# Expert layers: 16-bit one-hots laid out for adjacent pairs, and no tile of zeros

## The reference, cut to what matters

```python
def peer_ffn(x, w_q, sub_keys, exp_u, exp_v):
    q = (x @ w_q).reshape(B, T, PEER_HEADS, 2, PEER_DKEY // 2)
    s = jnp.einsum('bthcd,hcnd->bthcn', q, sub_keys)       # 8 heads, 2 sides, 128 keys
    top_s, top_i = lax.top_k(s, PEER_TOPK)                 # 16 of each side
    cand_s = top_s[..., 0, :, None] + top_s[..., 1, None, :]
    best_s, pos = lax.top_k(cand_s.reshape(..., 256), PEER_TOPK)
    idx = row * 128 + column                               # of the expert picked
    gate = jax.nn.softmax(best_s, axis=-1)
    h = jax.nn.gelu(jnp.einsum('md,mkd->mk', xb, exp_u[ib]))
    return jnp.einsum('mk,mkd->md', gb * h, exp_v[ib])     # 128 picks per token
```

## Time and profile before

| what | value |
|---|---|
| median of 3 runs | 3005.61 us |
| the runs | 3006.25, 2999.36, 3005.61 us |
| the profiled execution's own time | 2999.36 us |
| its span in the profile | 2997.6 us |
| PE busy, matmuls | 2594.2 us (87%) |
| PE busy, weight loads | 2419.3 us (81%) |
| DVE busy | 1988.2 us (66%) |
| ACT busy | 1347.4 us (45%) |
| POOL busy | 643.0 us (21%) |

### The profile page before, as it was taken

One profiled execution on the slowest core, in us unless ns is written; L12 is line 12 of the kernel. 1 busy time (PEld: TensorE's weight loads), 2 busy tenths in 40 slices (PEclk: granted clock), 3 DMA queues, 4 the chain that ended last, 5 costly groups with the idle time before them and its releaser, 6 DMA issues. The chain is left out here.

```text
span 2997.6 us, 61808 instructions
## 1 busy us (share of the span) xinstructions
PE 2594.2 (87%) x22240; PEld 2419.3 (81%) x22240; DVE 1988.2 (66%) x4119; ACT 1347.4 (45%) x2439; POOL 643.0 (21%) x506
## 2 busy tenths in 40 slices
PE   5798677798399589999999999866899999999998
PEld 2598556468397588999988899865899999988997
DVE  5501632341652469599999966546596899999765
ACT  5632334234320265655544455523555555444554
POOL 0144124227200379100000000162593000000000
PEclk9899779799696799999999999987999999999999
DMA  9522012115100234544434355421344544443452
GB/s 302 179 91 79 1 39 75 59 57 156 42 1 1 72 132 163 180 157 155 161 141 146 140 180 184 136 89 36 128 168 168 169 154 154 145 148 141 171 193 98
DMA packets 153851, 374.20 MB, mean 125 GB/s; under 512 B 8656, under 2 KB 102880, under 8 KB 137088
## 3 DMA queue, kind: packets, MB, share of 16 engines
q1 hardware_dynamic: 150784, 367.59, 36.1%
q10 hardware_dynamic: 2944, 4.98, 0.5%
HBM read 371.49 MB, written 1.05 MB: 124 GB/s over the span
## 5 line engine op out<-in xcount | busy, mean ns | idle before, releaser
L2413 ACT ACTIVATE w_hi<-ring 128x512 fp32r<-128x512 f32 x1024 | 643.6, 631 | 779.7 <-PE bank L2468 417.4
L2419 DVE TENSOR_TENSOR w_lo<-ring,w_hi 128x512 fp32r<-128x512 f32 x864 | 572.2, 690 | 207.7 <-ACT w_hi L2413 194.7
L360 POOL TENSOR_TENSOR w_lo<-ring,w_hi 128x512 fp32r<-128x512 f32 (+2 forms) x264 | 328.5, 1258 | 1340.4 <-ACT w_hi L351 1328.8
L2450 PE MATMUL bank<-x_hi,w_hi 128*128 128x256 f32 x2048 | 591.8, 289 | 20.4 <-POOL w_lo L2419 19.7
L2468 PE MATMUL bank<-hidden_hi,w_hi 128*128 128x256 f32 x2048 | 579.4, 283 | 34.3 <-issue 21.4
L2450 PE MATMUL bank<-x_lo,w_hi 128*128 128x256 f32 x2048 | 579.2, 283 | 0.0
L2450 PE MATMUL bank<-x_hi,w_lo 128*128 128x256 f32 x2048 | 578.9, 283 | 0.0
L2468 PE MATMUL bank<-hidden_hi,w_lo 128*128 128x256 f32 x2048 | 569.7, 278 | 0.0
L2468 PE MATMUL bank<-hidden_lo,w_hi 128*128 128x256 f32 x2048 | 569.2, 278 | 0.0
L2468 PEld LDWEIGHTS bank<-hidden_hi,w_hi 128*128 128x128 f32 x2048 | 383.8, 187 | 45.9 <-issue 29.9
L2450 PEld LDWEIGHTS bank<-x_hi,w_hi 128*128 128x128 f32 x2048 | 392.8, 192 | 24.2 <-ACT w_hi L2413 18.0
(11 more groups left out here) (519 smaller groups left out, 4460.8 us busy)
## 6 DMA issues: line engine op xcount, KB each, us to landing
ring<-in_peer_uT SPq DMA_DIRECT2D x128, 1024.0 KB, 4.9
ring<-in_peer_v SPq DMA_DIRECT2D x128, 1024.0 KB, 4.8
ring<-in_even_w_in SPq DMA_DIRECT2D x26, 1024.0 KB, 5.2
ring<-in_ada_w SPq DMA_DIRECT2D x24, 1024.0 KB, 8.8
ring<-in_odd_w_in SPq DMA_DIRECT2D x12, 1024.0 KB, 5.3
ring<-in_even_w_out SPq DMA_DIRECT2D x8, 1024.0 KB, 5.1
ring<-in_odd_w_out SPq DMA_DIRECT2D x8, 1024.0 KB, 5.1
ring<-in_peer_w_q SPq DMA_DIRECT2D x8, 1024.0 KB, 5.4
```

Source lines behind the costliest of these rows:

```text
L360: eng.tensor_tensor(k.lo[g % PARTS][:, 0:n], src, k.hi[g % PARTS][:, 0:n].bitcast(F32), ALU.subtract).then_inc(k.lo_ready, 1)
L2413: act.activation(k.hi[q][:, :], k.ring[slot][:, q * PART:q * PART + PART], ACT.Copy).then_inc(k.hi_ready, 1)
L2419: eng.tensor_tensor(k.lo[q][:, :], k.ring[slot][:, q * PART:q * PART + PART], k.hi[q][:, :].bitcast(F32), ALU.subtract).then_inc(k.lo_read ...
L2450: mm = pe.matmul(k.bank[s][:, j * T:j * T + T], a[q][:, w], b[:, cc, :], start=(cc == 0 and n == 0), stop=(cc == KC - 1 and n == 2))
```

## The change

It does six things.

1. `iota` moves from a tile of its own to the last 128 numbers of `hidden`. It is copied by DVE, once for each layer, to two bf16 tiles: `iota1` (0, 1, 2, ...) and `iota2` (0, 0, 1, 1, 2, 2, ...).
2. `rowT` holds each row index twice side by side. The one-hot of the row keeps its layout (token, row), and compares bf16 with bf16, with adjacent pairs innermost.
3. `hot` and `right` are laid out with the token innermost: (column, token) and (part, column, token). The one-hot of the column compares `iota2` with `colT`, pairs of tokens innermost.
4. `gateT` is laid out (part, token) and not (token, part).
5. PE's gate matmul takes as moving data `right[:, g, part, :, t]`: 64 columns, four elements (8 bytes) apart. Before they were adjacent.
6. The tile of zeros, its memset and the 16 matmuls of each layer are gone. The first matmul of each bank in column 0 of G2 starts the sum, the last of D ends it. For this the first round of G2 and the last of D are written out in place of a pass of the loop. DVE's last additions wait for `consumed`, the count of the parts that PE has used.

```diff
-        self.right = fold(small(2, GROUP, 3, HALF_J), "g t q j", g=2, t=GROUP, q=3)
-        self.hot = fold(small(GROUP, HALF_J), "t j", t=GROUP)
-        self.rowT, self.colT = small(T), small(T)
-        self.gateT = fold(small(T, 3), "t q", q=3)
-        self.zero = small(T)
+        self.right = fold(small(2, 3, HALF_J, GROUP), "g q j t", g=2, t=GROUP, q=3)
+        self.hot = fold(small(HALF_J, GROUP), "j t", t=GROUP)
+        self.rowT = fold(small(T, 2), "t c", c=2)
+        self.colT = small(T)
+        self.gateT = fold(small(3, T), "q t", q=3)
...
-                for a, b in ((k.hi, self.hh), (k.hi, self.hl), (k.lo, self.hh)):
-                    mm = pe.matmul(out, a[q][:, w], b[:, j, :], start=False, stop=False, skip_group_check=True)
+                for n, (a, b) in enumerate(((k.hi, self.hh), (k.hi, self.hl), (k.lo, self.hh))):
+                    mm = pe.matmul(out, a[q][:, w], b[:, j, :], start=first and cc % 2 == 0 and n == 0,
+                                   stop=last and cc % 2 == 1 and n == 2, skip_group_check=True)
...
-                mm = pe.matmul(k.bank[4 + g][:, t * HALF_J:(t + 1) * HALF_J], self.left[:, g, t, :], self.right[:, g, t, part, :],
+                mm = pe.matmul(k.bank[4 + g][:, t * HALF_J:(t + 1) * HALF_J], self.left[:, g, t, :], self.right[:, g, part, :, t],
...
-        self.zeros(pe, True)
-        with pe.Fori(0, ROUNDS) as r:
+        for n in range(STEPS):
+            self.dense_gates(pe, 2 * ROUNDS, n)
+            self.down_column(pe, 2 * ROUNDS, n // PAIR, n % PAIR, first=n == 0)
+        with pe.Fori(1, ROUNDS) as r:
...
-        with pe.Fori(0, ROUNDS) as r:
+        with pe.Fori(0, ROUNDS - 1) as r:
...
-        self.zeros(pe, False).then_inc(self.summed, 1)
+        for n in range(STEPS):
+            self.down_column(pe, 4 * ROUNDS - 1, n // PAIR, n % PAIR, last=n == STEPS - 1)
...
-        S.step(dve.tensor_copy(self.rowT[:, :], k.bank[6][:, 0:T]))
+        S.step(dve.tensor_copy(self.rowT[:, :, :], spread(k.bank[6][:, 0:T], 2, 2)))
...
-        j = self.iota[:, phase * HALF_J:(phase + 1) * HALF_J]
-        dve.tensor_tensor(self.hot[:, :, :], spread(j, 1, GROUP), spread(self.colT[:, at], 2, HALF_J), ALU.is_equal).then_inc(self.hot_ready, 1)
-        dve.tensor_tensor(self.left[:, g, :, :], spread(self.iota, 1, GROUP), spread(self.rowT[:, at], 2, P), ALU.is_equal)
+        j = self.iota2[:, phase * HALF_J:(phase + 1) * HALF_J, :]
+        hot = self.hot.rearrange("p j (a c) -> p j a c", c=2)
+        col = self.colT[:, at].rearrange("p (a c) -> p a c", c=2)
+        dve.tensor_tensor(hot, spread(j, 2, GROUP // 2), spread(col, 1, HALF_J), ALU.is_equal).then_inc(self.hot_ready, 1)
+        left = self.left[:, g, :, :].rearrange("p t (a c) -> p t a c", c=2)
+        i = self.iota1.rearrange("p (a c) -> p a c", c=2)
+        dve.tensor_tensor(left, spread(i, 1, GROUP), spread(self.rowT[:, at, :], 2, P // 2), ALU.is_equal)
         dve.wait_ge(self.hot_ready, r * STEPS + (phase * HALF_J + n + 1))
-        dve.tensor_tensor(self.right[:, g, :, :, :], spread(self.hot[:, :, :], 2, 3), spread(self.gateT[:, at, :], 3, HALF_J),
+        dve.tensor_tensor(self.right[:, g, :, :, :], spread(self.hot[:, :, :], 1, 3), spread(self.gateT[:, :, at], 2, HALF_J),
                           ALU.mult).then_inc(self.ready, 1)
...
-        k.dve.step(dve.memset(self.zero[:, :], 0.0))
+        k.dve.step(dve.tensor_copy(self.iota1[:, :], self.iota))
+        k.dve.step(dve.tensor_copy(self.iota2[:, :, :], spread(self.iota, 2, 2)))
...
-        dve.wait_ge(self.summed, 1)
+        dve.wait_ge(k.consumed, self.h0 + 4 * ROUNDS * ROUND * PARTS)
```

## The result

The changed kernel takes 3038.1 us (median of four runs, 3032.8 to 3038.7), the kernel before 3005.9 in the runs beside it. The ratio is 1.0105, with a 95% interval of 1.0093 to 1.0118. The change makes it 32 us slower. The forecast said 2952, with a range up to 3003; the first rival said 3041.

A forecast was written before the change was run, and what follows sets the result against it. PE was taken to bound G1 and D, DVE to bound G2. Savings of 50.7 (G2) + 2.2 (zeros) + 0.7 (start of G1) = 53.6 us gave 3005.6 - 53.6 = 2952.0 us, range 2932 to 3003.

The forecast's parts named there:

- the first rival: G1 and G2: stepped moving data slow PE's 12 gate matmuls to 0.71 us a group; 3041 us, chance 0.14.
- What bounds the stages: G1 is bound by PE at 3.32 us a step, G2 by DVE at 3.667, with PE's own step 3.27.
- DVE's 0.80 us: DVE's three one-hot instructions take half the time per element, saving 0.13 + 0.27 + 0.40 us a step.
- Half of it is slack: In G2 PE becomes the bound, so DVE's last 0.40 us a step buy nothing; `right` alone would do.
- The gate matmuls: PE's 12 per step in G1 and G2 stay at 30 ns each, 0.36 us, despite columns 8 bytes apart.
- The upper bound: Gate matmuls on PE: time goes with bytes passed over, 59 ns each, 0.35 us more a step.
- The rule that was weighed there: Gate matmuls' reads: two hits on a 16-byte SBUF line give full rate, so 8-byte steps cost nothing, right at the edge.
- no faster one-hots: Rival: DVE's one-hots don't get faster and G2 stays at 3.667 us a step; 3004 us, chance 0.07.
- a wait left in G2: Rival: `hidden_low` or a `w_hi` still comes last in part of G2's steps; 2977 us, chance 0.10.
- The zeros: Dropping them saves 0.2 us before G2 and about 0.9 us after D; 2.2 us over two layers.
- The start of G1: PE's one wait for `w_lo` there, 0.37 us once per layer, goes: 0.7 us saved.
- The two rhythms: Down stages run a matmul every 118 or 113 ns; the fast rhythm can give each of four stages 6.9 us.

The follow-up runs named there:

- adjacent reads: The changed kernel, but PE reads the same buffer as 64 adjacent columns, not 8 bytes apart (gates are then wrong numbers): 2954.8 us, ratio 0.9834.
- `right` alone: Against the pairs version, `hot` and `left` compare f32 again, so only `right` is made two elements at a time: 2955.7 us, ratio 0.9852.
- the sweeps: The kernel before with 12 extra matmuls ahead of each step's gate matmuls, operand steps varied: 64 bf16 columns 8 bytes apart took 58 ns a matmul.
- pairs version: The changed kernel with pairs of tokens innermost in the 16-bit one-hots, so PE reads columns 4 bytes apart: 2953.8 us, ratio 0.9828.

## Why the prediction was wrong

- **What bounds the stages: right.** G1 is PE's: with DVE idle for a fifth of it, it is still 3.32 us a step (adjacent reads). G2 was DVE's, and PE's own step there is 3.27 to 3.29 us, forecast 3.27.
- **DVE's 0.80 us: right**, 0.81. The rows of before only bounded it, and the forecast took the bound at half the time per element. The Trainium skill ("Vector Engine (DVE) Microarchitecture Reference", section 5.1) gives two elements a tick for such operands, also where a row of an input is read again at a step of 0. The trace agrees, with innermost runs of just two elements: 285, 419 and 552 ns are 0.13 us for each 256 elements more, and it was 0.27.
- **Half of it is slack: right.** With `right` alone the median is 1.9 us higher, and the steps of G2 account for 0.8 of it.
- **The gate matmuls: this step failed.** "I take 30: 64 columns of 2 bytes cost 0.47 ns each and 256 of 4 bytes 0.46, so that columns count and bytes don't." Measured: 57 ns. Both rows are adjacent data. In the sweeps 64 bf16 columns cost some 30 ns at a step of 2 bytes and of 4, so the first row lies at a floor, and a comparison of two adjacent reads says nothing of what a step adds. The upper bound, 59 ns by bytes passed over, came close for a reason that is not quite its own: up to 16 bytes the lines touched grow as the bytes do. The term, put at nothing, was 0.33 us a step. It put 42 us on G1 and took 41 from what G2 would have saved (the run with adjacent reads), because PE is the bound of both.
- **The rule that was weighed there.** The Trainium skill ("SBUF — State Buffer", "Door 1: The DMA port swizzle") gives two hits on a 16-byte line as enough for the full rate. The sweep has 58 ns for 64 columns with two hits on a line, 46 with 2.7, 31 with four. For TensorE's moving bf16 data the measurement decides: four hits are free, two cost double. Sixteen bytes fit as the unit, the threshold of two does not.
- **The first rival** gave 3041, with 0.71 us a group; 3038 and 0.69 were measured. It had 0.14, too little: no row of the kernel before had a stepped moving operand, and the reason against it was one comparison. The others, no faster one-hots and a wait left in G2, did not happen: PE is busy in all of G2.
- **The zeros: right in sum, with luck.** 2.2 us for 2.2, but the parts miss in opposite ways. Around G2's start, the last up matmul to the column went from 2.72 us (1499.35 to 1502.07) to 2.29 (1521.07 to 1523.36), and as much in layer 1: 0.4 where 0.2 was expected. After D, from the last matmul's start to DVE's first addition, it was 1.27 us in both layers, and is 0.39 in layer 0 and 0.77 in layer 1. So 0.9 and 0.5 us were saved where 0.9 each was expected. What delays the additions in layer 1 is open: it is 0.77 with adjacent reads and with pairs too, and 0.39 in the run with `right` only.
- **The start of G1: 1.2 us for 0.7.** From the first up matmul of a layer to the first gate matmuls it was 197.6 us and is 197.0, in both layers. The wait of PE for `w_lo`, 0.37 us, is gone; where the rest comes from is open.
- **The two rhythms** are not what decided, but bear on each comparison. The kernel before ran at 3006, 2999 and once 2991 us, steps of about 7 as forecast for one down stage; but I have traces of one execution each, so the link is an agreement, not shown. It isn't the only thing that varies: the execution traced with `right` only has both D stages at 118 ns and was still the fastest of its kernel, 2951.0, and its first up matmul starts at 1083.1 us where the other traces have 1087.9 to 1091.6. The pairs version has both D stages at 118 ns a matmul and 2953.8 us, where the sum for that case was 2952.0.

The forecast of 2952 was right for a kernel with PE's reads at their old price, 2954.8 with adjacent reads and 2953.8 with pairs, and wrong for this one.

## What to carry to other kernels

A layout that halves the time of the engine that writes can double that of the engine that reads: price both sides of a buffer, and the side that is the bound first. For bf16 moving data count the 16-byte lines that a matmul touches, some 1.8 ns each at a granted clock of 1.00; keep at least four columns on a line, as pairs of a two-element innermost run do, which was also all that VectorE needed here to take two elements at a time (`right` in 552 ns). Where no row of a profile shows an operand's form, put the weight of the forecast on the bound and not on a likeness, or measure the form with a few extra matmuls into an unused bank.

## What the runs showed of the hardware that was not expected

- Bf16 moving data: 1.7 to 1.9 ns for each 16-byte line touched, with a floor of 30 ns for 64 columns.
- Fp32r moving data: 0.47 ns a column for 256 adjacent ones, 0.84 for 128; 0.85 to 0.92 for either at steps of 8 to 64 bytes.
- Weights with a step are much cheaper than moving data with one: 128 columns 8 bytes apart 35 ns, 16 bytes apart 63 ns, and 64 at 32.
- DVE writing 768 2-byte results 8 bytes apart: 1945 ns, against 954 adjacent, with the same inputs.
- Down stages run at 118 or 113 ns a matmul at the same granted clock of 1.00, in one execution, for a whole stage each. It doesn't go by the layer: in the run where only PE's reading has the step, layer 0 has the 113. What sets the one or the other is open.
